# A two-layer mixture-of-experts model on one core: the token rows of an expert block picked by one-hot products on TensorE instead of stored to and gathered from device memory

## The reference, cut to what matters

```python
def _hier_moe(h, w_group, b_group, w_expert, b_expert, w_gate, w_up, w_down):
    ...                                    # router: 2 of 32 experts and their weights for each token
    A = T * MOE_TOP_K                      # 512 assignments of 256 tokens
    order = jnp.argsort(eid)
    e_s, tok_s, w_s = eid[order], tok[order], wts[order]
    ...
    xp = jnp.zeros((nb * MOE_BLOCK, D), h.dtype).at[dest].set(h[tok_s])   # rows of one expert side by side
    def expert_block(args):
        xb, e = args
        return (jax.nn.silu(xb @ w_gate[e]) * (xb @ w_up[e])) @ w_down[e]
    yp = lax.map(expert_block, (xp.reshape(nb, MOE_BLOCK, D), blk_e)).reshape(nb * MOE_BLOCK, D)
    return jax.ops.segment_sum(yp[dest] * w_s[:, None].astype(h.dtype), tok_s, num_segments=T)
```

## Time and profile before

| | us |
|---|---|
| median of 3 runs (lowest, highest) | 2458.9 (2455.12, 2461.4) |
| profiled execution: span from first to last instruction | 2451.3 |
| PE busy | 2077.8 (85%) |
| DVE busy | 1134.3 (46%) |
| ACT busy | 796.4 (32%) |
| POOL busy | 109.6 (4%) |
| weights requested by SyncE's queue (q1), share of 16 DMA engines | 57.9% |

### The profile page before, as it was taken

One profiled execution on the slowest core, in us unless ns is written; L12 is line 12 of the kernel. 1 busy time (PEld: TensorE's weight loads), 2 busy tenths in 40 slices (PEclk: granted clock), 3 DMA queues, 4 the chain that ended last, 5 costly groups with the idle time before them and its releaser, 6 DMA issues.

```text
span 2451.3 us, 46085 instructions
## 1 busy us (share of the span) xinstructions
PE 2077.8 (85%) x17112; PEld 1590.7 (65%) x17113; DVE 1134.3 (46%) x2111; ACT 796.4 (32%) x1534; POOL 109.6 (4%) x188
## 2 busy tenths in 40 slices
PE   7999778666768988655557999998999999998997
PEld 3567455434446955433334788886888788886886
DVE  4677211111115641111111666776666766867666
ACT  2233101000004420000000554554554554554554
POOL 0000100000000000000000000000000000000001
PEclk9999888888879988988888999999999999999999
DMA  9875899999997569999998755325546456334552
GB/s 391 325 287 190 329 414 421 414 424 429 419 376 282 192 257 409 424 428 421 422 422 360 274 185 171 137 93 172 172 153 209 153 160 193 132 117 142 173 157 83
DMA packets 277458, 668.86 MB, mean 273 GB/s; under 512 B 8656, under 2 KB 203216, under 8 KB 252240
## 3 DMA queue, kind: packets, MB, share of 16 engines
q1 hardware_dynamic: 264416, 532.99, 57.9%
q10 hardware_dynamic: 9360, 129.96, 12.6%
q0 software_dynamic: 3552, 4.20, 0.5%
HBM read 669.48 MB, written 3.15 MB: 274 GB/s over the span
## 4 chain that ended last, share of the span: by engine, by line
PE 70%; DMA 14%; another core or an unknown queue 6%; DVE 5%; issue 3%; ACT 2%; SPq 1%; POOL 0%; POOLq 0%; ACTq 0%; DVEq 0%; PEldq 0%
PE ps L2180 19%; PE ps L2185 10%; PE ps L1573 9%; DMA A<-in_moe_w_up 6%; PE ps L1598 4%; DMA ring<-in_moe_w_up 4%; PE ps L2454 4%; DMA arena<-f_rows,arena 3%; PE ps L1538 2%; PE ps L1545 2%; PE ps L2619 2%; PE ps L1983 1%; PE ps L1985 1%; PE ps L1984 1%
## 5 line engine op out<-in xcount | busy, mean ns | idle before, releaser
L2180 PE MATMUL ps<-XS,WS 128*128 128x512 f32 x1408 | 499.7, 399 | 8.9 <-DVE XS L689 7.8
L2165 DVE TENSOR_TENSOR WS<-ring,WS 128x1024 fp32r<-128x1024 f32 (+1 forms) x276 | 329.5, 1195 | 226.2 <-ACT WS L2160 225.8
L2185 PE MATMUL ps<-XS,WS 128*128 128x256 f32 x1408 | 396.7, 282 | 0.0
L2160 ACT CAST WS<-ring 128x1024 fp32r<-128x1024 f32 (+1 forms) x276 | 283.0, 1026 | 328.3 <-PE ps L2185 315.0
L1833 DVE TENSOR_TENSOR arena<-arena,ps 64x256 f32<-64x256 f32 x70 | 29.6, 424 | 706.8 <-ACT arena L1661 706.8
L2180 PEld LDWEIGHTS ps<-XS,WS 128*128 128x128 f32 x1408 | 265.4, 188 | 79.3 <-DVE XS L689 18.5
L2185 PEld LDWEIGHTS ps<-XS,WS 128*128 128x128 f32 x1408 | 268.0, 190 | 0.2 <-issue 0.2
L1573 PE MATMUL ps<-arena 128*32 128x256 f32 x1632 | 159.1, 460 | 109.4 <-DMA arena<-in_moe_w_up 74.3
L1573 PE MATMUL ps<-ring,arena 128*32 128x256 f32 x2240 | 160.6, 450 | 101.3 <-DMA ring<-in_moe_w_up 93.4
L2180 PE MATMUL ps<-HS,WS 128*128 128x512 f32 x616 | 216.4, 396 | 0.0
L1598 PE MATMUL ps<-ring,arena 128*32 128x256 f32 x2240 | 165.3, 445 | 54.8 <-DVE arena L1839 54.8
(11 more groups left out here) (352 smaller groups left out, 3212.4 us busy)
## 6 DMA issues: line engine op xcount, KB each, us to landing
ring<-in_moe_w_down ACTq DMA_DIRECT2D x60, 2048.0 KB, 14.4
ring<-in_ffn_w_gu SPq DMA_DIRECT2D x90, 1024.0 KB, 7.3
ring<-in_moe_w_gate SPq DMA_DIRECT2D x32, 2048.0 KB, 44.3
ring<-in_moe_w_up SPq DMA_DIRECT2D x32, 2048.0 KB, 52.4
arena<-in_moe_w_gate SPq DMA_DIRECT2D x32, 2048.0 KB, 44.3
ring<-in_w_mod SPq DMA_DIRECT2D x24, 2048.0 KB, 11.7
ring<-in_ffn_w_down SPq DMA_DIRECT2D x32, 1408.0 KB, 6.4
arena<-in_moe_w_up SPq DMA_DIRECT2D x16, 2048.0 KB, 53.0
```

The costliest lines, as they stand in the source:

```text
L2160: L.inc(L.eng.copy(self.parts(u)[0], source), self.w_high)
L2165: L.inc(L.eng.tensor_tensor(wl, self.unit(u)[1], high(wh), ALU.subtract), self.w_split)
L2180: L.eng.matmul(ps[:, bank, :].rearrange("p (j t) -> p j t", j=2), wh[:, i, :], moving[:, :, k, :], start=k == 0, stop=False)
L2185: mm = L.eng.matmul(ps[:, bank, 0:TL], wl[:, i, :], moving[:, 0, k, :], start=False, stop=k == total - 1)
```

## The change

The token rows stay on the chip. ACT copies them, in eight pieces of 128 x 256, from PSUM to the free half of `XT`. For each block DVE makes a 128 x 32 one-hot matrix `PICK` for each tile of tokens: `AT` holds for each assignment 32 x (block number - b) + place, `match` compares it with 0..31, `pick_matched` adds the two assignments of a token, and `shift` subtracts 32 for the next block. PE multiplies `PICK` with the token rows in four column groups (`pick_block`, 8 matmuls of 32 columns by 256), ACT copies the result (128 x 256: four row groups of 32 rows, each a quarter of the width) to `XG`, PE turns it with two transposes of 128 x 128 (`turn_block`), and ACT copies that to `XB` as before. POOL's gathers, index copies and waits go, as do the store to `f_rows`, the integer table and the seven products that kept PE busy. SyncE waits for `ranges` (the blocks of each expert, now written right after the first `PICK`) instead of the table. The table is still made, since the results' way back to the tokens needs it; it now comes after the pick and turn of block 0, in PSUM bank 7.

The diff, cut to its core:

```diff
@@ class Moe: tiles
-    self.XG = take(D)
+    self.AT = take(2 * NT)
+    self.MATCH = take(2 * NT * CAP).rearrange("p (c t a) -> p c t a", c=2, t=NT)
+    self.PICK = take(NT * CAP).rearrange("p (t a) -> p t a", t=NT)
+    self.XG = take(D // 4)
...
-    self.ROWS = [arena[:, rows_at + i * D:rows_at + (i + 1) * D] for i in range(2)]
+    self.ROWS = [XT[:, 4 * t:4 * t + 4, TL:TA] for t in range(NT)]
...
@@ Moe.pe
+    def pick_block():
+        for t in range(NT):
+            for q in range(4):
+                mm = pe.matmul(ps[self.lane_rows(q), 3, TL:TA], self.PICK[:, t, :], self.ROWS[t][:, q, :],
+                               start=t == 0, stop=t == NT - 1)
+        mm.then_inc(self.picked.sem, 1)
+    def turn_block():
+        for i in range(2):
+            mm = pe.transpose(ps[:, 3, i * P:(i + 1) * P], self.XG[:, i * P:(i + 1) * P], IDENT)
+        mm.then_inc(self.block_turned.sem, 1)
+    zeros = self.YS.bitcast(BF16)
+    L.wait(self.rows_kept, NT)
+    pe.wait_ge(self.picks.sem, 1)
+    pick_block()
+    pe.wait_ge(self.y_kept.sem, 1)
+    for bank in (1, 4, 5, 6):
+        pe.matmul(ps[:, bank, :], zeros[:, 0:P], zeros[:, 0:512], start=True, stop=False)
+    pe.wait_ge(self.picked_kept.sem, 1)
+    turn_block()
     for t in range(NT):
         for c in range(2):
             L.wait(self.places, 2 * t + c + 1)
-            mm = pe.matmul(ps[:, 6, 0:2 * NB], self.AT_PLACE[t][c],
+            mm = pe.matmul(ps[:, 7, 0:2 * NB], self.AT_PLACE[t][c],
                            self.AT_BLOCK[t][c].rearrange("p c b -> p (c b)"),
                            start=t + c == 0, stop=2 * t + c == 2 * NT - 1)
     L.inc(mm, self.table)
...
-    def turn_block():
-        for c in range(KD):
-            mm = pe.transpose(ps[:, 3, c * CAP:(c + 1) * CAP], by_eight[:, c, :], IDENT[0:CAP, 0:CAP])
-        mm.then_inc(self.block_turned.sem, 1)
-    zeros = self.YS.bitcast(BF16)
-    L.wait(self.rows_kept, NT)
-    pe.wait_ge(self.y_kept.sem, 1)
-    for bank in (1, 4, 5, 6):
-        if bank == 6:
-            L.wait(self.table_kept, 2)
-        pe.matmul(ps[:, bank, :], zeros[:, 0:P], zeros[:, 0:512], start=True, stop=False)
-    keep_busy(L, 7, 7)
-    pe.wait_ge(self.gathered.sem, 16)
-    turn_block()
...
+                x = self.XB[:, k % 2 * P + k // 2 * CAP:k % 2 * P + (k // 2 + 1) * CAP]
                 for q in range(4):
                     weight = (gate, up)[q // 2][:, k, q % 2 * HALF_FF:(q % 2 + 1) * HALF_FF]
                     mm = pe.matmul(ps[self.lane_rows(q), 0, 0:HALF_FF], x, weight, start=k == 0, stop=k == KD - 1)
             mm.then_inc(self.hidden.sem, 1)
-            pe.wait_ge(self.gathered.sem, b * 16 + 32)
+            pe.wait_ge(self.picks.sem, b + 2)
             pe.sem_inc(spare.sem, 1)
-            turn_block()
+            pick_block()
...
+            pe.wait_ge(self.picked_kept.sem, b + 2)
+            pe.sem_inc(spare.sem, 1)
+            turn_block()
...
+    L.wait(self.ranges, 1)
...
@@ Moe.act
-        if t >= 2:
-            L.wait(self.rows_out[t % 2], 16)
-        L.inc(act.copy(self.ROWS[t % 2], ps[:, 1 + 2 * (t % 2):3 + 2 * (t % 2), :].rearrange("p b n -> p (b n)")),
-              self.rows_kept)
-        L.join()
-        act.dma_start(f_rows[t * P:(t + 1) * P, :], self.ROWS[t % 2]).then_inc(self.rows_out[t % 2].sem, 16)
+        for q in range(4):
+            rows = ps[:, 1 + 2 * t:3 + 2 * t, :].rearrange("p b n -> p (b n)").rearrange("p (n c) -> p c n", c=KD)
+            L.inc(act.copy(self.ROWS[t][:, q, :].rearrange("p (i n) -> p i n", i=2), rows[:, 2 * q:2 * q + 2, :]),
+                  self.rows_kept if q == 3 else None)
...
-    for t in range(2, NT):
-        store_rows(t)
     load_table(L, ACT.Silu)
-    L.wait(self.table_kept, 1)
+    def keep_picked():
+        act.copy(self.XG, ps[:, 3, TL:TA]).then_inc(self.picked_kept.sem, 1)
     def keep_tokens():
-        act.copy(self.XB.rearrange("p c a -> p (c a)"), ps[:, 3, 0:8 * CAP]).then_inc(self.x_kept.sem, 1)
+        act.copy(self.XB, ps[:, 3, 0:KD * CAP]).then_inc(self.x_kept.sem, 1)
+    act.wait_ge(self.picked.sem, 1)
+    keep_picked()
     act.wait_ge(self.block_turned.sem, 1)
     keep_tokens()
+    L.wait(self.ranges, 1)
...
+            act.wait_ge(self.picked.sem, b + 2)
+            keep_picked()
...
-    L.wait(self.gathered_all, 1)
...
@@ Moe.dve
+    step(v.scalar_tensor_tensor(out=self.AT, in0=self.BLK, scalar=float(CAP), in1=self.RANK, op0=ALU.mult, op1=ALU.add))
+    def match():
+        return v.tensor_tensor(self.MATCH.rearrange("p c t a -> p (c t) a"),
+                               IOTA[:, 0:CAP].unsqueeze(1).to_broadcast([P, 2 * NT, CAP]),
+                               self.AT.unsqueeze(2).to_broadcast([P, 2 * NT, CAP]), ALU.is_equal)
+    def shift():
+        return v.tensor_scalar(self.AT, self.AT, -float(CAP), None, ALU.add)
+    def pick_matched():
+        return v.tensor_tensor(self.PICK, self.MATCH[:, 0], self.MATCH[:, 1], ALU.add)
+    step(match())
+    pick_matched().then_inc(self.picks.sem, 1)
+    L.inc(shift())
+    L.inc(v.tensor_copy(self.FIRSTI, self.FIRST), self.ranges)
...
-    step(v.tensor_copy(self.FIRSTI, self.FIRST))
-    L.wait(self.table, 1)
-    tab = ps[:, 6, 0:2 * NB].rearrange("p (c b) -> p c b", c=2)
-    step(v.tensor_scalar(self.EMPTY, tab[:, 1, :], 0.5, OUT_OF_BOUNDS, ALU.is_lt, ALU.mult))
-    step(v.scalar_tensor_tensor(out=self.TABI, in0=tab[:, 1, :], scalar=-1.0, in1=self.EMPTY, op0=ALU.add, op1=ALU.add),
-         self.table_kept)
-    step(v.tensor_copy(self.TAB, tab), self.table_kept)
     for t in range(NT):
         L.inc(v.tensor_scalar(self.TOKEN[:, t * P:(t + 1) * P], IOTA, float(t * P + 1), None, ALU.add))
     L.join()
+    step(match())
+    v.wait_ge(self.picked.sem, 1)
+    pick_matched().then_inc(self.picks.sem, 1)
+    shift().then_inc(self.shifted.sem, 1)
+    L.wait(self.table, 1)
+    tab = ps[:, 7, 0:2 * NB].rearrange("p (c b) -> p c b", c=2)
+    step(v.tensor_copy(self.TAB, tab), self.table_kept)
...
+            v.wait_ge(self.shifted.sem, b + 1)
+            match().then_inc(self.matched.sem, 1)
+            v.wait_ge(self.picked.sem, b + 2)
+            v.sem_inc(spare.sem, 1)
+            v.wait_ge(self.matched.sem, b + 1)
+            pick_matched().then_inc(self.picks.sem, 1)
+            shift().then_inc(self.shifted.sem, 1)
...
@@ Moe.pool
-    for i in range(2):
-        L.wait(self.rows_out[i], 16 * (NT // 2))
-    g.memset(self.XG, 0.0).then_inc(self.index_g.sem, 1)
     g.memset(self.COMBINE, 0.0).then_inc(self.combine_made.sem, 1)
-    L.wait(self.table_kept, 1)
...
-    with g.Fori(0, blocks) as b:
-        g.wait_ge(self.gathered.sem, b * 16 + 32)
-        g.wait_ge(self.block_turned.sem, b + 2)
-        g.sem_inc(spare.sem, 1)
-        gather(bass.ds(b + 2, 1), b + 2)
...
@@ sync
-    sp.wait_ge(moe.table_kept.sem, moe.table_kept.base + 1)
+    sp.wait_ge(moe.ranges.sem, moe.ranges.base + 1)
```

More of the change, by code:

```diff
@@ L46 @@
 HALF_FF = FF // 2
-OUT_OF_BOUNDS = 4096.0
 LAYERS = 2
@@ L252, in carver @@
             return take
-        f_rows = nc.dram_tensor("f_rows", [TL, D], F32, kind="Internal").ap()
         const_in = sig("const_in")
@@ L1392, in __init__ @@
                 self.table = shared("moe_table", 1)
-                self.table_kept = shared("moe_table_kept", 2)
+                self.table_kept = shared("moe_table_kept", 1)
                 self.combined = shared("moe_combined", 2)
-                self.gathered_all = shared("moe_gathered_all", 1)
+                self.ranges = shared("moe_ranges", 1)
                 self.x_added = shared("moe_x_added", KD)
                 self.next_norm = norms[2 * l + 2]
-                self.rows_out = [shared(f"moe_rows_out{i}", 16 * NT // 2) for i in range(2)]
+                self.picks = sig(f"moe{l}_picks")
+                self.matched = sig(f"moe{l}_matched")
+                self.shifted = sig(f"moe{l}_shifted")
+                self.picked = sig(f"moe{l}_picked")
+                self.picked_kept = sig(f"moe{l}_picked_kept")
                 self.block_turned = sig(f"moe{l}_block_turned")
@@ L1446, in __init__ @@
                 self.TAB = take(2 * NB).rearrange("p (c b) -> p c b", c=2)
[L1447 to L1449 removed]
                 self.YS = take(D // 4)
                 self.LIMITS = take(TL // CAP - 1)
[L1453 to L1454 removed]
+                self.AT = take(2 * NT)
+                self.MATCH = take(2 * NT * CAP).rearrange("p (c t a) -> p c t a", c=2, t=NT)
+                self.PICK = take(NT * CAP).rearrange("p (t a) -> p t a", t=NT)
+                self.XG = take(D // 4)
                 self.SG, self.H = take(HALF_FF), take(HALF_FF)
[L1456 removed]
+                self.XB = take(KD * CAP)
                 self.HB = take(FT * CAP).rearrange("p (c t) -> p c t", c=FT)
                 self.COMBINE = take(TL)
[L1459 to L1460 removed]
+                self.ROWS = [XT[:, 4 * t:4 * t + 4, TL:TA] for t in range(NT)]
+                assert take.used() <= EXTRA_AT, take.used()
```

(27 more changed lines are left out.)

9 lines of the change are left out of this document (removed).

## The result

In alternating runs on one chip the kernel before took 2457.0 us (median of 4, 2454.8 to 2461.4) and the kernel after 2387.5 us (median of 4, 2386.8 to 2391.5): ratio 0.9714, 95% interval 0.9691 to 0.9736, or 69.5 us less. The forecast was 46 us less, with a range that ended at 2403: the direction was right, the size was not. The profiled execution took 2387.1 us with a span of 2385.3, so that its own time stands only 1.8 us above the span; the prediction had kept a distance of 7.6 us.

What follows compares the result with a forecast made beforehand. The DMA engines were taken to set the time in the loops. Gains of 14.0 + 7.3 + 11.6 + 13.0 = 45.9 us off the 2451.3 span gave 2405.4, with the median's 7.6 kept 2413; range 2403 to 2436.

Steps and rivals of the forecast that it cites:

- distance of 7.6 us: Whole program: the runs' median lies 7.6 us above the profiled span, and the forecast keeps this.
- What bounds the kernel: Expert loops: the saturated DMA engines set the time; product, gather or turn is waited for only in the first few blocks.
- Term 1: Start of each mixture's loop: an earlier block 0 brings expert 4's request forward, gaining 14.0 and 7.3 us.
- The clock: First products without fillers: wholly at half the clock, they cost 1.4 and 2.4 us more, giving 2417.
- Term 2: Saturated stretches: removing 70 gathers frees their share of DMA time, 11.6 us if spread evenly over the engines.
- Term 3: Ends of both mixtures' weights: gather rows load the 16 engines unevenly; removing them gains 6.5 us each, 13 together.
- even gathers: Ends of the mixtures: the engines' lag has another cause, so unevenness gains 0; 2426 us, chance 0.24.
- more: Ends' lag goes fully (+3.1 us) and first blocks run at full clock (+3.5); 2406 us, chance 0.10.
- The start stays: Loop start: something else holds block 0 back as long as the gather did; only 24.6 us gained, 2434, chance 0.08.
- PE becomes the bound: Loop: at half clock a block takes 16.0 us on PE against 15.2 per expert; 2480 us, chance 0.03.

Runs made afterwards that it cites:

- e11: Kernel after with the next block's turn put in front of the combine instead of behind it: 2393.1 us, ratio 0.9733.
- e7: Kernel before with only the first two gathers of each mixture issued, so its output is not the reference's: 2410.9 us, ratio 0.9823.
- e8: Kernel after with the seven filler products put back before the first block of each mixture: 2398.4 us, ratio 0.9766.
- e6: Kernel after plus an unused 32-row gather per block, first 16 rows valid, written into partitions 0, 4, ..., 124: 2403.4 us, ratio 0.9797.
- e3: Kernel after plus an unused 32-row gather per block with all indices out of range: 2389.3 us, ratio 0.9715.
- e9: Kernel before with gathers into partitions 0, 4, ..., 124 and the turn reading them by products with every fourth identity column: 2568.6 us, ratio 1.0444.
- e1: Kernel after plus an unused 32-row gather per block, first 16 rows valid, into partitions 0 to 31: 2437.4 us, ratio 0.9912.
- e15: Kernel after plus an unused 32-row gather per block, first 16 rows valid, landing in partitions 32, 35, ..., 77: 2433.1 us, ratio 0.9901.
- e14: Kernel after plus an unused 32-row gather per block, only even rows valid, landing in partitions 0, 8, ..., 120: 2410.1 us, ratio 0.9800.
- e4: Kernel after plus 16 unused plain rows per block by ScalarE's hardware queue into partitions 0 to 15: 2438.6 us, ratio 0.9923.
- e10: Kernel after plus 16 unused plain rows per block by ScalarE's hardware queue into partitions 0, 2, ..., 30: 2426.9 us, ratio 0.9860.
- e13: Kernel after plus 16 unused plain rows per block by ScalarE's hardware queue into partitions 0, 4, ..., 60: 2416.8 us, ratio 0.9825.
- e5: Kernel after plus 16 unused plain rows per block by ScalarE's hardware queue into partitions 0, 8, ..., 120: 2417.9 us, ratio 0.9844.
- e2: Kernel after plus an unused 32-row gather per block, only even rows valid, landing in partitions 0, 2, ..., 30: 2420.6 us, ratio 0.9852.

## Why the prediction was right in direction and wrong in size

**What bounds the kernel** was read rightly: with the DMA engines full, e11's longer blocks cost 5 us, and both kernels without the loop's gathers (after and e7) gained.

**Term 1, the start (21.3 us predicted): right.** Block 0's product began at 263.3 on the old clock, forecast 263.5; in it the pick took 1.57 (1.7), the range loads 1.65 (2.7) and the table 1.03. Measured: 14.6 us in the first mixture (14.0), 7.9 in the second (7.3), 22.5 together. One half was right for a wrong reason: the request moved by 17.8 us, not by 14.0. Two products before it ran at the full clock and brought the rest: the first product in 3.66 us, where it had taken 5.48, and the first down product in 1.93, where the prediction kept 3.61. The surplus bought nothing, since the idle stretch had ended with less; what counted was the idle time of the engines (12.1 us) and the store. e8 shows from the other side what the start is worth: a first product 5.3 us later in the first mixture, a request for expert 4 that is 9.0 us later in the second, and with them 13 us in all.

**The clock.** The Trainium skill (TensorE: Matmul & The Clock Gate, Part 1) says that the throttled clock is the default and activity releases it. The prediction took that as speaking against taking the fillers away, and priced it at 3.8 us. This cost did not come: the first product ran 3.66 us in both mixtures, 5.48 and 3.66 with the fillers. The granted clock over 300 to 700 us rose from 0.84 to 0.89; that is not due to the fillers' absence, since e8 has them and 0.89 too.

**Term 2, the gathers' own share (11.6): right for what it counts.** e6 shows 12 us for as many rows.

**Term 3, unevenness (13.0): right.** Without gathers the ends are gone; with e6's rows 13.4 us of them are back. The rival "even gathers" (2426) falls by that. The Trainium skill (DMA: Bandwidth & Descriptors, Latency and other measured facts) says that two of the sixteen engines are usually slower, with the descriptor rings of GpSimd's DMAs as its best guess of the cause. e3 issues a gather once a block without a valid row and costs 0.2 us (give or take 6), so here it is the rows, not the rings.

**The step that failed** is the sentence "70 of them lie in saturated stretches: 11.6 us", which charged the gathers with their own packets' time alone. The prediction said that what shares the saturated engines costs in full; it cost more. The 4 KB rows also lengthened the weights' packets: 2.392 us per megabyte with them, 2.338 without, 21.7 us over both mixtures. Put in as a fourth term, it makes the sum 22.5 + 11.6 + 13.0 + 21.7 = 68.8, against 70.2 by the stage lengths and 69.5 by the medians. A sign was in the trace before. Three stretches of 100 us in it, each saturated, that differ in the number of gathers (POOL's count is two to a gather, so 9, 7.5 and 6):

```profile
320.00:420.00 100.00, 79.00 (x1096) 50.54 (x1088) 13.72 (x44) 10.09 (x27) 9.82 (x18) 0.88 1.01 416
420.00:520.00 100.00, 69.64 (x884) 43.46 (x888) 11.59 (x37) 7.84 (x21) 7.88 (x15) 0.83 1.01 419
520.00:620.00 100.00, 64.25 (x804) 39.25 (x800) 9.49 (x30) 7.10 (x19) 6.64 (x12) 0.83 1.01 426
```

Three gathers more took 10 of 426 GB/s, or 2.3 us of the 100: 0.8 us a gather, where the prediction's own share is 12.3 / 74 = 0.17. Seventy of them by this reading are 55 us; 47.7 were measured. It is no more than a sign: in the second mixture the same division gives 423, 424 and 423 GB/s for 8, 6.5 and 6.5 gathers per 100 us (960 to 1260 us), where the slope does not show. The range ended at 2403, because its best case still knew only the ends and the clock, and no bound was put on a slowdown of the neighbours. The distance of 7.6 us between span and median, 2.2 in the kernel after, cancels in the forecast gain of 45.9 us; the kernel before itself came out 1.9 us lower (2457.0) than the 2458.9 from which the forecast started.

**Rivals.** The conditions of "more" (2406) came true, short ends and first products at the full clock, and it was still 18 us too high, since it lacked the same term. "The start stays" is refuted by the trace of after; "PE becomes the bound" did not happen here, and e9 shows that it was three microseconds a block away.

## What to carry to other kernels

Where DMA engines are saturated, price a small transfer by what it does to the large ones too: compare the time per megabyte of the main queues in stretches with and without it, and ask into which partitions its rows go. Here some 60 KB of rows per block beside 6 MB per expert cost 48 us in 2457, of which only 12 were their own. And products that keep an engine busy belong where a wait hides them: with the wait gone, they cost 13 us here.

## What the runs showed of the hardware

- 4 KB rows written into partitions 0 to 15 beside 16 KB weight rows cost over three times their own time (e1: 49 us over after, own share 0.6% of 2436, 15 us). The same rows into partitions 0, 4, ..., 60 cost 20 us (e6), and into 32, 35, ..., 77 again 46 us (e15). In the single packet records over 300 to 680 us the weights' 16 KB packets took a mean of 611 ns in after, e6 and e14, and 627, 632 and 634 ns in before, e1 and e15; a 4 KB row itself took 160 ns in e6 and 181 in e1.
- A hardware queue's rows are no cheaper: 51, 36, 27 and 32 us over after for 16 rows at distances 1, 2, 4 and 8 (e4, e10, e13, e5).
- An indirect gather of 32 rows, all out of range, once a block cost 0 us, give or take 6 (e3).
- How a gather's rows are shared out over the DMA engines went with their destination: the same sixteen even rows left half of the engines' time idle in the last ten us of a mixture's weights when written to partitions 0, 8, ..., 120 (share 0.49, e14), and hardly any when written to 0, 2, ..., 30 (share 1.00 until 4.7 us before the end, e2).
- f32 products whose moving operand takes every fourth column of the identity were dear as a turn: 16 instructions with 128 rows took 4.03 us, 0.25 us each, where 32-row transposes took 0.89 for seven (e9).
